# Retention values of heads 1 to 3 as seven block products instead of eight

## The reference, cut to what matters

```
def retention_mixer(h, w_in, out_g, w_out):            # h: 512 tokens x 1024
    proj = h @ w_in                                    # q, k: 4 heads x 256; v: 4 heads x 512; gate: 2048
    q = rotary(q) ; k = rotary(k) * 256 ** -0.5
    v = proj[..., 2048:4096].reshape(bsz, seq, 4, 512)
    ret = decayed (q k^T) v per head                   # chunked in the reference, as a whole in the kernel
    y = rms_norm(ret) * silu(g)
    return y @ w_out
```

## Time and profile before

| | |
|---|---|
| median of 3 runs | 2100.87 us |
| lowest, highest | 2100.79, 2102.26 us |
| the profiled execution's own time | 2100.51 us |
| its span, first to last instruction | 2098.7 us |
| granted TensorE clock | 1.00 |
| busy: PE, DVE, ACT, POOL | 2079.6, 1436.8, 1135.1, 1213.0 us |
| instructions on PE | 11739 matmuls |

### The profile page before, as it was taken

One profiled execution on the slowest core, in us unless ns is written; L12 is line 12 of the kernel. 1 busy time (PEld: TensorE's weight loads), 2 busy tenths in 40 slices (PEclk: granted clock), 3 DMA queues, 4 the chain that ended last, 5 costly groups with the idle time before them and its releaser, 6 DMA issues.

```text
span 2098.7 us, 31298 instructions
## 1 busy us (share of the span) xinstructions
PE 2079.6 (99%) x11739; PEld 1815.0 (86%) x11739; DVE 1436.8 (68%) x2363; ACT 1135.1 (54%) x1874; POOL 1213.0 (58%) x757
## 2 busy tenths in 40 slices
PE   9999999999999999999999999999999999999999
PEld 7867889889898989888899898888887888899998
DVE  7973886767586666776776684897577325885773
ACT  6564654654553536456646544446877435645642
POOL 3514666874686657645658844655433554838843
PEclk9999999999999999999999999999999999999999
DMA  4203233333323132232233325322222243333232
GB/s 168 71 11 96 94 94 101 101 101 109 117 62 116 62 105 77 94 98 91 91 101 105 107 89 182 101 81 81 71 62 70 95 138 91 101 101 101 91 109 93
DMA packets 57685, 200.79 MB, mean 96 GB/s; under 512 B 6400, under 2 KB 7168, under 8 KB 57280
## 3 DMA queue, kind: packets, MB, share of 16 engines
q1 hardware_dynamic: 56816, 197.46, 29.7%
q10 hardware_dynamic: 720, 1.34, 0.2%
HBM read 194.32 MB, written 4.19 MB: 95 GB/s over the span
## 4 chain that ended last, share of the span: by engine, by line
PE 58%; DVE 2%; ACT 1%; issue 1%; ACTq 0%; DVEq 0%
PE ps L421 13%; PE ps L422 13%; PE ps L423 13%; PE ps L724 5%; PE ps L726 5%; PE ps L725 5%; PE ps L451 1%; PE ps L449 1%; PE ps L450 1%; PE ps L2789 1%; PE ps L2774 0%; PE ps L2801 0%; DVE G L1851 0%; PE ps L2776 0%; PE ps L2798 0%
## 5 line engine op out<-in xcount | busy, mean ns | idle before, releaser
L399 POOL TENSOR_TENSOR WL<-WS,WH 128x1024 fp32r<-128x1024 f32 (+1 forms) x248 | 586.6, 2369 | 537.8 <-ACT WH L389 537.2
L421 PE MATMUL ps<-H,WH 128*128 128x512 f32 (+2 forms) x1264 | 493.0, 390 | 2.3 <-DVE H L629 1.8
L422 PE MATMUL ps<-H,WH 128*128 128x512 f32 (+2 forms) x1264 | 490.7, 388 | 0.0
L423 PE MATMUL ps<-H,WL 128*128 128x512 f32 (+2 forms) x1264 | 490.5, 388 | 0.0
L1236 POOL TENSOR_TENSOR WL<-WS,WH 128x512 fp32r<-128x512 f32 x232 | 311.8, 1357 | 243.2 <-ACT WH L847 241.7
L389 ACT ACTIVATE WH<-WS 128x1024 fp32r<-128x1024 f32 (+2 forms) x250 | 256.9, 1030 | 169.9 <-PE ps L423 87.9
L421 PEld LDWEIGHTS ps<-H,WH 128*128 128x128 f32 (+1 forms) x1264 | 237.0, 188 | 52.0 <-issue 3.1
L423 PEld LDWEIGHTS ps<-H,WL 128*128 128x128 f32 (+1 forms) x1264 | 236.9, 187 | 49.4
L422 PEld LDWEIGHTS ps<-H,WH 128*128 128x128 f32 (+1 forms) x1264 | 237.1, 188 | 46.2
L421 PE MATMUL ps<-G,WH 128*128 128x512 f32 x496 | 193.8, 391 | 2.8 <-DVE G L2508 1.4
L422 PE MATMUL ps<-G,WH 128*128 128x512 f32 x496 | 193.1, 389 | 0.0
(11 more groups left out here) (378 smaller groups left out, 4811.8 us busy)
## 6 DMA issues: line engine op xcount, KB each, us to landing
WS<-in_w SPq DMA_DIRECT2D x337, 512.0 KB, 3.5
WS<-in_w SPq DMA_DIRECT2D x24, 384.0 KB, 3.0
xs<-X SPq DMA_DIRECT2D x1, 2048.0 KB, 6.9
X<-xs SPq DMA_DIRECT2D x8, 256.0 KB, 3.7
out<-X SPq DMA_DIRECT2D x8, 256.0 KB, 2.0
X<-in_sg SPq DMA_DIRECT2D x1, 1344.0 KB, 5.8
X<-in_x ACTq DMA_DIRECT2D x4, 256.0 KB, 5.8
X<-in_x SPq DMA_DIRECT2D x4, 256.0 KB, 5.5
```

The source lines that it names most:

```text
L399: e.tensor_tensor(lo, raw, hi.bitcast(F), ALU.subtract).then_inc(*P.sig("w_lo", i))
L421: e.matmul(out, lh, rh, start=start, stop=False)
L422: e.matmul(out, lh, rl, start=False, stop=False)
L423: return e.matmul(out, ll, rh, start=False, stop=stop)
```

## The change

For heads 1, 2 and 3 the values are made by seven products of half-size blocks. Weights come in four units by blocks: 256 of the 512 columns, and the even or the odd rows of 128 features; that is 1024 columns per unit, as before in size. The names are a11, a21, a22, a12 for units 0 to 3. DVE makes four sums of them, each of 1024 columns (s1 = a21 + a22, s2 = s1 - a11, s4 = a12 - s2, s3 = a11 - a21 in the place of a21). s1 and s4 are written to `SQ`, s2 to `TMP`. The stationary operand is a block of `H` (for a11, s4 and a12) or of the turned rows (for s1, s2, s3 and a22), 128 tokens at a time, the moving operand 256 columns of the weight sums. A product is 24 matmuls (two blocks of tokens, four rows of features, three passes), all seven are 168 matmuls of 256 columns. Parts of results that are needed twice are copied out of PSUM by ACT (six copies of 128 x 256) and added back by DVE (six additions of 128 x 256). All seven weight operands go through a pair of cells and so through one ACT cast and one POOL subtraction of 1024 columns each; before there were four of each. Head 0 stays as it was.

```
-            u["bv", h, v] = [("b_w_in", 0, k, 2048 + 512 * h, 512) for k in (2 * v, 2 * v + 1)]
+            if h in V_PAIRED:                       # (1, 2, 3)
+                half, odd = ((0, 0), (1, 0), (1, 1), (0, 1))[v]
+                u["rv", h, v] = [("b_w_in", 0, k, 2048 + 512 * h + 256 * half, 256) for k in range(odd, 8, 2)]
...
-PAIRED_UNITS = ("dns", "ups", "rp")
+PAIRED_UNITS = ("dns", "ups", "rp", "rv")
...
+    if key[0] == "rv":                              # when a place of WS may be loaded again
+        return [[("w_lo", (key[0:2], "a11")), ("r_sum", (key[0:2], "s3"))], [("w_lo", (key[0:2], "s3"))],
+                [("w_lo", (key[0:2], "a22"))], [("w_lo", (key[0:2], "a12")), ("r_sum", (key[0:2], "s4"))]][second]
...
+V_ORDER = ("a11", "s1", "s2", "s4", "s3", "a22", "a12")
...
+def pe_value_pair(P, e, h):
...
+    def product(name, b, out, first, ready=None):
+        key = (pair, name)
+        hi, lo = P.cell(key, NXW)
+        if ready:
+            e.wait_ge(*P.at(*ready))
+        if b == 0:
+            e.wait_ge(*P.at("w_lo", key))
+        for q in range(4):
...
+            w = slice(256 * q, 256 * q + 256)
+            e.matmul(out, rh, hi[:, w], start=first and q == 0, stop=False, skip_group_check=True)
+            e.matmul(out, rh, lo[:, w], start=False, stop=False, skip_group_check=True)
+            t = e.matmul(out, rl, hi[:, w], start=False, stop=q == 3, skip_group_check=True)
...
+    for b in range(2):
+        product("a11", b, chain[b], True)
+    for b in range(2):
+        product("s1", b, right[b], True)
+    for b in range(2):
+        product("s2", b, chain[b], False, ("ct", (pair, "p1", b)))
+    for b in range(2):
+        product("s4", b, right[b], False, ("ct", (pair, "p5", b)))
+    for b in range(2):
+        product("s3", b, chain[b], False, ("ct", (pair, "u2", b)))
+    for b in range(2):
+        product("a22", b, chain[b], False, ("c22", (pair, b)))
+        product("a12", b, left[b], False)
...
 (ACT, head h)
+            value_part(h, "p1")
+            value_forms(h, "s4")
+            value_part(h, "p5")
+            value_forms(h, "s3")
+            value_part(h, "u2")
+            value_forms(h, "a22", "a12")
+            forms(one, "a11", "s1")
+            value(h, 2)
+            value(h, 3)
+            forms(one, "s2")
+            value(h, 0)
+            value(h, 1)
+            forms(one, "a12")
...
 (ACT, end of head h, behind the casts of bout)
         for mp in range(1 if h == 2 else 4):
             cast(("bout", h, mp))
...
+        if h + 1 in V_PAIRED:
+            value_forms(h + 1, "a11", "s1", "s2")
...
 (DVE, head h)
+            value_sum(h, "s4")
+            value_sum(h, "s3")
+            value_c(h, "c12", 0)
+            value_c(h, "c12", 1)
+            value_c(h, "c22", 0)
+            e.wait_ge(*P.at("w_lo", (("rv", h), "s4")))
+            sums(one, "s1")
+            value_c(h, "c22", 1)
...
 (DVE, end of head h)
         for mp in range(1 if h == 2 else 4):
+            if h + 1 in V_PAIRED and mp == (0 if h == 2 else 2):
+                value_sum(h + 1, "s1")
+            if h + 1 in V_PAIRED and mp == 3:
+                value_sum(h + 1, "s2")
...
+        if h == 2 and h + 1 in V_PAIRED:
+            value_sum(h + 1, "s2")
...
 (POOL, head h)
-        units(("bv", h, 3))
+        if h in V_PAIRED:
+            for name in V_ORDER:
+                key = (("rv", h), name)
+                hi, lo = P.cell(key, NXW)
+                e.wait_ge(*P.at("w_hi", key))
+                e.tensor_tensor(lo, v_raw(P, h, name) if name[0] == "a" else v_sum(P, h, name), hi.bitcast(F),
+                                ALU.subtract).then_inc(*P.sig("w_lo", key))
```

More of the change, by code:

```diff
@@ L1400, in pe_row_pair, with v_raw, v_raw_in, v_sum @@
     P.cell_n += 1
+V_ORDER = ("a11", "s1", "s2", "s4", "s3", "a22", "a12")
+def v_raw(P, h, name):
+    i = P.index.get(("rv", h, ("a11", "a21", "a22", "a12").index(name)), 0)
+    return P.m["WS"][:, i % STAGE * NXW:i % STAGE * NXW + NXW]
+def v_raw_in(P, h, name):
+    i = P.index.get(("rv", h, ("a11", "a21", "a22", "a12").index(name)), 0)
+    return f"w_in{i % STAGE}", i
+def v_sum(P, h, name):
+    return {"s1": P.m["SQ"][:, 0:NXW], "s2": P.m["TMP"][:, 0:NXW], "s3": v_raw(P, h, "a21"), "s4": P.m["SQ"][:, 0:NXW]}[name]
@@ new lines, in v_part @@
+def v_part(P, name, b):
+    return r_sil(P, ("p1", "u2", "p5").index(name))[:, 256 * b:256 * b + 256]
+def pe_value_pair(P, e, h):
+    pair = ("rv", h)
+    for z in range(4):
+        listed(P, ("rv", h, z))
+    o = [bank(P, e, (("bv", h), j), True) for j in range(4)]
+    for name in V_ORDER:
+        cells(P, (pair, name), 2)
+    def product(name, b, out, first, ready=None):
[6 more added lines that the diff above has]
+        for q in range(4):
+            if name in ("a11", "a12", "s4"):
+                k, c = 2 * q + (name != "a11"), slice(256 * (name == "s4") + 128 * b, 256 * (name == "s4") + 128 * b + 128)
+                rh, rl = P.H(k, 0)[:, c], P.H(k, 1)[:, c]
+            else:
+                form, c = {"s1": "t1", "s2": "t2", "s3": "t3", "a22": "t4"}[name], slice(128 * b, 128 * b + 128)
+                rh, rl = r_tx(P, q, 0, form)[:, c], r_tx(P, q, 1, form)[:, c]
+            w = slice(256 * q, 256 * q + 256)
+            e.matmul(out, rh, hi[:, w], start=first and q == 0, stop=False, skip_group_check=True)
+            e.matmul(out, rh, lo[:, w], start=False, stop=False, skip_group_check=True)
+            t = e.matmul(out, rl, hi[:, w], start=False, stop=q == 3, skip_group_check=True)
+        t.then_inc(*P.sig("prod", (pair, name, b)))
+        P.end["cell", key] = ("prod", (pair, name, 1))
+    chain, left, right = [o[b][:, 256:512] for b in range(2)], [o[b][:, 0:256] for b in range(2)], [o[b + 2][:, 0:256] for b in range(2)]
+    for b in range(2):
[11 more added lines that the diff above has]
+        product("a12", b, left[b], False)
+    for j in range(4):
+        drop(P, (("bv", h), j))
@@ L1416, in pe_ret @@
     for h in range(4):
-        for _ in tokens(P, e, ("bv", h), [("bv", h, u) for u in range(4)]):
-            pass
+        if h in V_PAIRED:
+            pe_value_pair(P, e, h)
+        else:
+            for _ in tokens(P, e, ("bv", h), [("bv", h, u) for u in range(4)]):
+                pass
         for j in range(4):
@@ L1520, in part, with value_forms, value_part, value @@
         e.activation(dst, src, ACT.Copy).then_inc(*P.sig("ct", (pair, name)))
+    def value_forms(h, *names):
+        for name in names:
+            key = (("rv", h), name)
+            if name[0] == "a":
+                e.wait_ge(*P.at(*v_raw_in(P, h, name)))
+            else:
+                e.wait_ge(*P.at("r_sum", key))
+            for u in P.cell_before[key]:
+                e.wait_ge(*P.freed("cell", u))
+            e.activation(P.cell(key, NXW)[0], v_raw(P, h, name) if name[0] == "a" else v_sum(P, h, name),
+                         ACT.Copy).then_inc(*P.sig("w_hi", key))
+            if name == "a12":
+                P.hi_n = P.index.get(("rv", h, 3), 0) + 1
+    def value_part(h, name):
+        for b in range(2):
+            j, c, ready = {"p1": (b, slice(256, 512), "a11"), "p5": (b + 2, slice(0, 256), "s1"),
+                           "u2": (b, slice(256, 512), "s2")}[name]
+            e.wait_ge(*P.at("prod", (("rv", h), ready, b)))
+            e.activation(v_part(P, name, b), P.ps((("bv", h), j))[:, c], ACT.Copy).then_inc(*P.sig("ct", (("rv", h), name, b)))
+    def value(h, j):
+        if h in V_PAIRED:
+            e.wait_ge(*P.at(*(("c11", (("rv", h), j)) if j < 2 else ("c22", (("rv", h), j - 2)))))
+            if j >= 2:
+                e.wait_ge(*P.at("c12", (("rv", h), j - 2)))
+        else:
+            e.wait_ge(*P.at("tok", (("bv", h), 3, j)))
+        if h and j == 2:
+            e.wait_ge(*P.at("ret", (h - 1, 3)))
+        e.activation(r_v(P, j, 0), P.ps((("bv", h), j)), ACT.Copy).then_inc(*P.sig("v_hi", (h, j)))
     def decayed(h, j):
@@ L1553, in act_ret @@
         q, k = ("qk", 2 * h + 2), ("qk", 2 * h + 3)
-        cast(("bv", h, 0))
-        if h == 0:
+        if h in V_PAIRED:
+            value_part(h, "p1")
[11 more added lines that the diff above has]
+            forms(one, "a12")
+        else:
+            cast(("bv", h, 0))
             qk_split(0, 1)
             turned_hi(2)
-        cast(("bv", h, 1))
-        if h == 0:
+            cast(("bv", h, 1))
             turned_hi(3)
[L1561 to L1568, removed]
+            cast(("bv", h, 2))
+            cast(("bv", h, 3))
+            forms(one, "a11", "s1", "s2", "a12")
+            for j in range(4):
+                value(h, j)
         forms(one, "s3")
@@ L1727, in gate @@
             e.wait_ge(*P.at("y_norm", (h - 1, j)))
+        if h in V_PAIRED and j < 3:
+            e.wait_ge(*P.at(("c11", "c12", "c22")[j], (("rv", h), 1)))
         e.tensor_tensor(r_sil(P, j), P.ps(key), r_scale(P), ALU.mult).then_inc(*P.sig("r_gate", (h, j)))
```

(31 more changed lines are left out.)

45 lines of the change are left out of this document (added).

## The result

| | before | after |
|---|---|---|
| median, us | 2100.81 (14 runs) | 2105.03 (14 runs) |
| lowest to highest, us | 2100.64 to 2102.46 | 2104.81 to 2106.49 |
| profiled execution, span / own time, us | 2098.7 / 2100.51 | 2103.1 / 2104.91 |

A forecast was written before the change was run, and what follows sets the result against it. The prediction took the columns PE streams to bound the kernel. Matmuls saved in three heads (-4.8 us) and head 3's wait (+8.6) make +3.8, so 2104.7 us against the median 2100.87; range 2101.5 to 2109.0.

The forecast's parts named there:

- PE's gain: Values of heads 1 to 3: 20.15 us of matmuls replace 21.76, 1.61 us less per head, 4.8 in all.
- Heads 1 and 2 have the head start: Outputs still running on PE let operands be ready in time; nothing waits, 0.5 us to spare at the tightest.
- rival B: Heads 1 and 2 also wait for DVE and POOL, 1.0 to 2.0 us per head: 2106.7 to 2108.7; chance 0.14.
- Head 3's long wait: Ahead of head 3's values PE waits 6.8 us for a11, cast and split behind the copies of q and k.
- Rival C: Head 3 doesn't wait, as a11's low part is there by 846.25; all three heads gain: 2096.1; chance 0.06.
- The two waits behind: Within head 3's values PE waits 0.5 us for s1's low part and 1.3 more for s4's.
- The term of 8.6: Head 3's whole wait: 6.8 ahead of its values plus 0.5 and 1.3 within them, 8.6 us.
- Rival A: TensorE's clock falls to half in head 3's long wait: 2105.7, or 2108.6 with two slow products; chance 0.28.
- The +1.0 us: Price of the fallen clock if head 3's first product runs slow: s4 starts at 864.6 instead of 863.6.
- The sum: Whole kernel: -4.8 us of matmuls plus 8.6 us of waiting in head 3 gives +3.8 us.
- the line of 0.2%: Whole kernel time: the least difference told from no change, 0.2% or 4.2 us, so 2105.1; slower 0.53, same 0.42.

The follow-up runs named there:

- e1: The change in heads 1 and 2 alone, head 3 with the code of the kernel before: 2097.83 us, ratio 0.9985.
- e2: The change in head 3 alone, the other heads with the code of the kernel before: 2108.23 us, ratio 1.0034.
- e4: The changed kernel with head 3's cast of a11 moved ahead of the four copies of q and k on ACT: 2106.76 us, ratio 1.0025.
- e7: The changed kernel with head 3's s1 and s2 summed ahead of the rotation, and a11, s1, s2 cast ahead of the copies: 2106.43 us, ratio 1.0025.
- e3: The changed kernel with 28 unread matmuls of 512 columns ahead of head 3's first product, to keep TensorE busy: 2105.67 us, ratio 1.0022.
- e5: The changed kernel with head 3's four weight sums made on 8 of their 1024 columns: 2104.34 us, ratio 1.0017.
- e6: The changed kernel with head 3's sums on 8 columns and 26 unread matmuls ahead of its values: 2104.04 us, ratio 1.0013.

## Why the prediction was right, point by point

**PE's gain.** 20.15 us per head were worked out and 20.15 measured in heads 1 and 2; e1 gives them alone, −2.9 for −3.2.

**Heads 1 and 2 have the head start.** PE waits nowhere in them, so rival B is out. The low part of s2 in head 1 ends at 668.60 + 2.89 = 671.49, worked out as 671.5. The tightest step is a12: its low part ends at 680.11 + 2.40 = 682.51, worked out as 682.4, and PE starts its product at 683.03, which leaves 0.5 us as worked out (POOL twice, then PE):

```profile
668.60 2.89 POOL L2111 TENSOR_TENSOR WL<-TMP,WH 128x1024 fp32r<-128x1024 f32 x1 [1.16 <-ACT WH L1615]
...
680.11 2.40 POOL L2111 TENSOR_TENSOR WL<-WS,WH 128x1024 fp32r<-128x1024 f32 x1 [0.27 <-ACT WH L1615]
```

```profile
683.03 0.28 PE L1461 MATMUL ps<-WH,H 128*128 128x256 f32 x1
```

**Head 3's long wait.** With the 2.84 us by which PE comes earlier than in before (843.41 for 846.25), the steps were: cast of a11 at 845.76 (845.74), low part done at 850.06 (849.91), wait 6.8 (6.65). Its cause is the order on ACT and DVE: e2 has it alone, e4 and e7 move it. Rival C, in which the cast goes first, was false in the order, and e4 shows that even with the cast first it brings nothing: a11 was there, and the wait stood ahead of s1. That all three heads would gain as soon as a11 is in time was wrong as a condition.

**The two waits behind.** 0.5 and 1.3 us were expected. In after they are 1.5 us of slow columns in the first product and 0.16 ahead of s4; in e3, at full clock, they are 0.22 and 1.06. The low part of s4 ends at 860.25, worked out as 860.7. The term of 8.6 measured 28.58 − 20.15 = 8.4, of which 6.65 + 1.53 + 0.16 = 8.3 stand in these places.

**Rival A: the rule was right, its price wasn't.** The clock fell, as the Trainium skill says of an idle TensorE (TensorE: Matmul & The Clock Gate, Part 1); the rows of after agree, with a granted clock of 0.50 from 847 to 853. The +1.0 us didn't come: the rival's step let the whole first product run slow, 5.76 us, and it took 4.41. That is 1.5 more than at full clock, where waits of 0.22 + 1.06 = 1.3 stood anyway. e3 shows the price as zero in the profiled execution; e5 with e6 shows 1.6, and the same is worked out from the rows of e4, where the low clock lasts longer than the lack of operands.

**What was small or open.** The sum was +3.8 and 4.2 to 4.4 were measured. Head 3 came 0.2 us better than worked out; 0.4 between and ahead of the heads and 0.4 in the tail came on top, no step of the prediction, and what causes these wasn't tried. So the total came out by two misses of opposite sign, each under 1 us. The measured value lies on the line of 0.2%, and so doesn't say which side of it deserved the higher chance.

## What to carry over

Columns taken off TensorE are worth their time only where the preparation of the new operands, which the other engines do, has a head start; before spending DVE and POOL work on fewer columns, count for each place how many microseconds of TensorE's own work stand between the last obstacle on those engines and the first product. Where that head start is missing, moving a cast or a sum forward can merely move the wait, as each move holds something else: the two reorderings here (e4, e7) brought nothing, with D 2.1 and 1.0 us longer. Whether the lack is one of work alone isn't shown: two orders were tried, and in one of them DVE also stood idle for weights. Before putting a sum ahead, look when its weights land. The better answer was to make the change only where the head start is: in heads 1 and 2 alone, 2097.8 us against 2100.7 and 2105.0.

## What the runs showed of the hardware

- The clock fell 3.1 us behind the end of the last matmul in after (843.4, 846.5), 3.6 in e4 (846.25, 849.8) and 3.7 in e5 (844.9, 848.6). It was back 3.3 us behind the start of the next matmul in after (850.06, 853.4), 4.6 in e5 (850.83, 855.5) and 6.0 in e4 (854.06, 860.1), with matmuls end to end in between. The times of change are worked out from the granted clock of windows of 1 us: for after 0.77 from 846 to 847 and 0.81 from 853 to 854. The same low clock can thus cost 1.5 us of columns (4.41 for 2.88, after) or 2.7 (862.54 for 859.82, e4).
- At low clock the 256-column matmuls of the first product start 213 ns apart (850.41, 850.62, 850.84), against 120 at full clock: 1.8 times, not twice.
- A DVE sum of 8 columns takes 0.15 us when POOL is idle, and 2.22 when a low part runs (timeline of DVE in e5):

```profile
853.15 2.22 DVE L1869 TENSOR_TENSOR SQ<-WS,TMP 128x8 f32<-128x8 f32 x1 [2.44 <-POOL WL L2112]
855.30 0.15 DVE L1864 TENSOR_TENSOR WS<-WS 128x8 f32<-128x8 f32 x1
```

It waited for its turn, not for its work, which bears out the reading of one of the two at a time.

- That reading holds for DVE operations with both operands in SBUF. Those with one in PSUM aren't held: the rotation's L1834 (`SC<-ps,SC`) takes 0.67 us at 835.78 in after, while POOL works, and 0.69 at 841.49, when it doesn't; the multiplication of two SBUF operands takes 2.50 and 0.68.
